# RWKV chunks of a hybrid decoder step: Z and Y formed transposed, group norm by sums on TensorE

## The reference, cut to what matters

```python
def step(state, inp):                       # wkv_scan
    r_t, w_t, k_t, v_t, kk_t, a_t = inp
    s_kk = jnp.einsum('bhvk,bhk->bhv', state, kk_t)
    state = (state * w_t[:, :, None, :] - s_kk[..., None] * (kk_t * a_t)[:, :, None, :]
             + v_t[..., None] * k_t[:, :, None, :])
    return state, jnp.einsum('bhvk,bhk->bhv', state, r_t)
...
mu = jnp.mean(y, axis=-1, keepdims=True)    # over the 64 values of a head
var = jnp.mean(jnp.square(y - mu), axis=-1, keepdims=True)
y = ((y - mu) * lax.rsqrt(var + GN_EPS)).reshape(bsz, t, D_RWKV)
y = y * lw['ln_x_w'].astype(f32) + lw['ln_x_b'].astype(f32)
```

## Time and profile before

| What | Value |
|---|---|
| median of three runs | 2047.21 us |
| the profiled execution's own time | 2051.09 us |
| its span | 2049.3 us |
| TensorE busy, weight loads | 1964.9 us (96%), 1821.8 us (89%) |
| VectorE, ScalarE, GpSimd busy | 988.7 us (48%), 625.6 us (31%), 201.8 us (10%) |
| mean granted TensorE clock | 0.987 |

### The profile page before, as it was taken

One profiled execution on the slowest core, in us unless ns is written; L12 is line 12 of the kernel. 1 busy time (PEld: TensorE's weight loads), 2 busy tenths in 40 slices (PEclk: granted clock), 3 DMA queues, 4 the chain that ended last, 5 costly groups with the idle time before them and its releaser, 6 DMA issues.

```text
span 2049.3 us, 40598 instructions
## 1 busy us (share of the span) xinstructions
PE 1964.9 (96%) x16426; PEld 1821.8 (89%) x16426; DVE 988.7 (48%) x1541; ACT 625.6 (31%) x991; POOL 201.8 (10%) x177
## 2 busy tenths in 40 slices
PE   7999999999999997998898999999999999999997
PEld 7997679999999997965667999999999999999996
DVE  6556766666666665156875644322132222213334
ACT  5114333333332322254545533321032112102213
POOL 0000212222222221221110000000000000000000
PEclk9999999999999998999999999999999999999998
DMA  4213722112232217476564621111111111111112
GB/s 174 84 39 119 262 51 55 49 47 54 60 78 70 74 56 195 150 239 199 167 234 144 232 100 43 50 41 51 42 41 51 41 51 41 45 47 42 51 42 84
DMA packets 111971, 189.45 MB, mean 92 GB/s; under 512 B 62871, under 2 KB 66231, under 8 KB 110407
## 3 DMA queue, kind: packets, MB, share of 16 engines
q1 hardware_dynamic: 109542, 179.15, 27.5%
q10 hardware_dynamic: 2304, 8.50, 1.3%
HBM read 149.83 MB, written 37.79 MB: 92 GB/s over the span
## 4 chain that ended last, share of the span: by engine, by line
PE 72%; issue 14%; DVE 8%; DMA 2%; ACT 2%; POOL 1%; SPq 1%; ACTq 0%; DVEq 0%; POOLq 0%
PE ps L294 44%; PE ps L384 5%; PE ps L386 4%; PE ps L385 4%; PE ps L1022 2%; PE ps L1023 1%; PE ps L1053 1%; DVE arena L1916 1%; DVE arena L1909 1%; PE ps L1210 1%; PE ps L1314 1%; PE ps L1269 1%; DMA normed<-in_kp 1%; PE ps L1136 1%; PE ps L1328 1%
## 5 line engine op out<-in xcount | busy, mean ns | idle before, releaser
L294 PE MATMUL ps<-h_high,wb_split 128*128 128x350 f32 (+1 forms) x1536 | 290.6, 324 | 0.0
L294 PE MATMUL ps<-ff_high,wb_split 128*128 128x350 f32 x1488 | 280.2, 323 | 0.0
L304 ACT CAST wb_split<-weights 128x1024 fp32r<-128x1024 f32 x88 | 92.3, 1049 | 592.7 <-PE ps L294 592.7
L294 PEld LDWEIGHTS ps<-h_high,wb_split 128*128 128x128 f32 x1536 | 254.5, 189 | 0.4
L294 PEld LDWEIGHTS ps<-ff_high,wb_split 128*128 128x128 f32 x1488 | 246.7, 189 | 0.0
L2248 DVE TENSOR_TENSOR arena<-arena,ps 128x1050 f32 (+1 forms) x39 | 48.7, 1249 | 311.1 <-PE ps L294 311.1
L294 PE MATMUL ps<-ff_low,wb_split 128*128 128x350 f32 x744 | 160.6, 324 | 0.0
L2329 POOL TENSOR_TENSOR arena<-arena,constants 64x512 f32<-64x512 f32 x100 | 121.7, 1217 | 332.0 <-DVE arena L1909 322.1
L386 PE MATMUL ps<-fill_high,w_fill_low 128*128 128x350 f32 x468 | 153.4, 328 | 0.0
L2265 DVE SCALAR_TENSOR_TENSOR squares<-ps,arena 128x1050 f32<-128x1050 f32 x32 | 40.1, 1253 | 220.1 <-PE ps L294 209.7
L294 PEld LDWEIGHTS ps<-ff_low,wb_split 128*128 128x128 f32 x744 | 127.0, 189 | 0.0
(11 more groups left out here) (348 smaller groups left out, 3682.4 us busy)
## 6 DMA issues: line engine op xcount, KB each, us to landing
weights<-in_wu SPq DMA_DIRECT2D x122, 512.0 KB, 3.5
normed<-in_vp SPq DMA_DIRECT2D x64, 260.0 KB, 4.6
normed<-in_kp SPq DMA_DIRECT2D x64, 256.0 KB, 4.9
arena<-chunk_dram SPq DMA_DIRECT2D x10, 1248.0 KB, 6.9
arena<-gate_dram SPq DMA_DIRECT2D x16, 525.0 KB, 4.0
chunk_dram<-arena SPq DMA_DIRECT2D x12, 520.0 KB, 5.1
chunk_dram<-fox SPq DMA_DIRECT2D x12, 520.0 KB, 4.6
arena<-samp_dram SPq DMA_DIRECT2D x10, 512.0 KB, 10.6
```

The costliest lines, as they stand in the source:

```text
L294: last = pe.matmul(PS[:, 3 * s + g, 0:n], ws[s][wh][:, k * P:(k + 1) * P], tile_of(x[xh], k)[:, g * G:g * G + n], start=(k == 0 and wh + x ...
L304: act.copy(of[0][s][0], W[:, s]).then_inc(w_hi[s], 1)
```

## The change

Z and Y of a head pair are formed together and transposed (values on partitions). V (104x64) stands and both blocks of MK (208 columns) move; the state stands and [a, r] (208 columns) moves; the two heads of a pair write the two halves of the partitions. Z is copied out (`ZT`) and transposed back to rows in level 4 for u. Y stays in its bank, NU stands and MB1 moves on top of it. Group norm works on transposed Y: ScalarE copies it, TensorE sums over each head's 64 partitions with the block of ones `blk` (416 columns), VectorE centers and squares, TensorE sums again, ScalarE takes Ln and Exp of all 128x416, VectorE scales. `y_back` is gone. The banks of the levels' products move (2, 3 to 4, 5; 4, 5 to 0, 1), because 2 and 3 now hold Z and Y. Two filler steps move from ahead of u to behind it, four stand between the sums, the last four behind them.

```diff
-        Yc = Xm.rearrange("p a b -> p (a b)")
-        gst = r_c2.take(4, NH)
+        ZT, YS_c, SQ_c, RS_c = Lm, E3, Lm, Lc
...
+        LEVELS, ZN_LV = range(1, N_LV), N_LV - 3
...
+                def zy_out(rows, p, x=slice(0, 2)):
+                    at = p % 2 * 2 * C
+                    return PS[rows, 2 + p // 2, at + x.start * C:at + x.stop * C]
+
-                if c:
-                    fill.run(4)
-                    y_back(c - 1)
-                fill.run(12 if c else 8)
+                fill.run(16 if c else 8)
...
                 for h, e, p, rows in by_rows():
-                    pe.matmul(z_out(e, p), MK[0:C, h, 0], Vn[0:C, vcols(h)], start=(p == 0), stop=False,
+                    pe.matmul(zy_out(rows, p), Vn[0:C, vcols(h)], MK[0:C, h].rearrange("p x t -> p (x t)"),
+                              start=(p % 2 == 0), stop=False, skip_group_check=True)
                 for h, e, p, rows in by_rows():
-                    last = pe.matmul(z_out(e, p), AR[rows, p, 0], St[rows, p], start=False, stop=(p == HP - 1),
+                    last = pe.matmul(zy_out(rows, p), St[rows, p], AR[rows, p].rearrange("p a b -> p (a b)"),
+                                     start=False, stop=(p % 2 == 1), skip_group_check=True)
...
+                    if lv == ZN_LV:
+                        wait(ch_act, "z")
+                        wait(ch_dve, f"x_{lv - 1}_0_x")
+                        for p in range(HP):
+                            last = pe.transpose(PS[0:C, 4, p * P:(p + 1) * P], ZT[:, p], ident)
+                        ch_pe.done(last, "zn")
...
+                def head_sums(src):
+                    for e in range(2):
+                        rows = slice(e * HD, (e + 1) * HD)
+                        last = pe.matmul(PS[rows, 0, 0:HP * C], blk[rows, rows],
+                                         src[rows].rearrange("p a b -> p (a b)"), start=True, stop=True)
+                    return last
...
-                fill.run(2)
-                wait(ch_act, "z")
+                wait(ch_act, "zn")
                 wait(ch_dve, f"x_{N_LV - 1}_1_xt")
...
                 ch_pe.done(last, "u")
-                for h, e, p, rows in by_rows():
-                    pe.matmul(y_out(e, p), AR[rows, p, 1], St[rows, p], start=(p == 0), stop=False,
-                for h, e, p, rows in by_rows():
-                    pe.matmul(y_out(e, p), MK[0:C, h, 1], Vn[0:C, vcols(h)], start=False, stop=False,
-                fill.run(2)
-                wait(ch_act, "nu")
-                for h, e, p, rows in by_rows():
-                    last = pe.matmul(y_out(e, p), MB[0:C, h, 1], NU[0:C, h * HD:(h + 1) * HD], start=False,
-                ch_pe.done(last, "y")
+                fill.run(4)
                 for h, e, p, rows in by_rows():
                     pe.matmul(s_out(rows, p), Kn[0:C, vcols(h)], Vn[0:C, vcols(h)], start=(p == 0), stop=False,
+                wait(ch_act, "nu")
+                for h, e, p, rows in by_rows():
+                    last = pe.matmul(zy_out(rows, p, slice(1, 2)), NU[0:C, h * HD:(h + 1) * HD], MB[0:C, h, 1],
+                                     start=False, stop=True, skip_group_check=True)
+                ch_pe.done(last, "y")
...
                 ch_pe.done(last, "s")
+                wait(ch_act, "y")
+                ch_pe.done(head_sums(YS_c), "mean")
+                fill.run(4)
+                wait(ch_dve, "sq")
+                ch_pe.done(head_sums(SQ_c), "var")
                 fill.run()
-                if c == NC - 1:
-                    y_back(c)
```

On ScalarE and VectorE:

```diff
+                act.wait_ge(ch_act.sem, ch_act.before(c))
...
-                ch_act.done(act.copy(Zm[0:C].rearrange("p (e n) -> p e n", e=2), PS[0:C, 2:4, 0:HP * HD]), "z")
+                ch_act.done(act.copy(ZT.rearrange("p (b a) t -> p b a t", b=2), zy_part(0)), "z")
...
+                    if lv == ZN_LV:
+                        wait(ch_pe, "zn")
+                        ch_act.done(act.copy(Zm[0:C], PS[0:C, 4, :]), "zn")
...
+                wait(ch_pe, "y")
+                ch_act.done(act.copy(YS_c.rearrange("p (b a) t -> p b a t", b=2), zy_part(1)), "y")
+                wait(ch_pe, "var")
+                ch_act.done(act.activation(RS_c.rearrange("p a b -> p (a b)"), PS[:, 0, 0:HP * C], ACT.Ln,
+                                           scale=1.0 / HD, bias=par[:, V_GEPS:V_GEPS + 1]), "ln")
                 wait(ch_act, "ln")
+                ch_act.done(act.activation(RS_c, RS_c, ACT.Exp, scale=-0.5), "rstd")
                 out(5)
...
-                wait(ch_pe, "yt")
+                wait(ch_dve, "norm")
                 for p in range(HP):
-                    ch_act.done(act.activation(YTc[:, p], PS[:, 0, p * C:(p + 1) * C], ACT.Identity,
+                    ch_act.done(act.activation(YTc[:, p], YS_c[:, p], ACT.Identity,
...
-                wait(ch_pe, "y")
-                done(dve.tensor_reduce(gst[0:C, 0].rearrange("p (e a) -> p e a", e=2), y, AX.X, ALU.add), "sum")
-                done(dve.tensor_scalar(gst[0:C, 0], gst[0:C, 0], 1.0 / HD, None, ALU.mult), "mean")
+                wait(ch_pe, "mean")
+                done(dve.scalar_tensor_tensor(YS_c, PS[:, 0, 0:HP * C].rearrange("p (a b) -> p a b", a=HP), -1.0 / HD,
+                                              YS_c, ALU.mult, ALU.add), "center")
+                done(dve.tensor_tensor(SQ_c, YS_c, YS_c, ALU.mult), "sq")
                 wait(ch_pe, "s")
...
-                done(dve.tensor_tensor(ych, y, spread4(0), ALU.subtract), "center")
-                done(dve.tensor_tensor(by_head(Zm[0:C]), ych, ych, ALU.mult), "sq")
...
                 wait(ch_act, "rstd")
-                done(dve.tensor_tensor(ych, ych, spread4(3), ALU.mult), "norm")
+                done(dve.tensor_tensor(YS_c, YS_c, RS_c, ALU.mult), "norm")
```

More of the change, by code:

```diff
@@ L597, in build @@
                       + [f"prod_{m}{i}" for i in range(2) for m in "kb"] + ["z"]
[L598 to L601, removed]
+                      + [x for lv in LEVELS for t in ("t1", *(("zn",) if lv == ZN_LV else ()),
+                                                      *(("t2x",) if lv < N_LV - 1 else ()),
+                                                      *(("t2",) if lv >= N_LV - 2 else ()))
+                         for x in ([t] if t == "zn" else [f"{t}_{lv}_{q}" for q in range(2)])]
+                      + ["u", "y", "s", "mean", "var"])
         ch_act = Steps(sem("ch_act"), ["v", "e1", "e3", "e2", "nat_k", "z"]
-                       + [f"t1_{lv}_{q}" for lv in LEVELS for q in range(2)]
-                       + ["nu", "ln", "rstd"] + [f"y_{p}" for p in range(HP)])
+                       + [x for lv in LEVELS for x in [f"t1_{lv}_{q}" for q in range(2)] + ["zn"] * (lv == ZN_LV)]
+                       + ["nu", "y", "ln", "rstd"] + [f"y_{p}" for p in range(HP)])
         ch_dve = Steps(sem("ch_dve"), [f"scan_{p}" for p in range(HP)] + ["lm", "r", "k", "b", "a", "nat_b", "nat_v"]
@@ L610, in build @@
                                           for t in (("xt", "xl") if lv == N_LV - 2 else ("xt",))])]
-                       + ["sum", "mean", "state_sum", "state", "center", "sq", "var", "norm"])
+                       + ["center", "sq", "state_sum", "state", "norm"])
         ch_pool = Steps(sem("ch_pool"), [f"bm_{lv}_{b}" for lv in LEVELS[:-1] for b in ("top", "low")] + ["bonus", "gate"])
@@ L770, in _ @@
             sp.dma_start(A["o_sp"], St).then_inc(sp_stored, 16)
+            sp.wait_ge(ch_act.sem, ch_act.before(NC))
             sp.dma_start(dS.rearrange("p b h k -> p (b h k)"), A["st"]).then_inc(ds_load, 16)
@@ L990, in _ @@
             pe.sem_inc(ch_pe.sem, 1)
[L992 to L996, removed]
             def pe_chunk(c):
@@ L1081, in pe_chunk @@
                     for q in range(2):
-                        wait(ch_act, f"t1_{lv}_{q}")
+                        wait(ch_act, "zn" if lv == ZN_LV else f"t1_{lv}_{q}")
                         if lv > 1:
@@ L1094, in pe_chunk @@
                     for j in range(4):
-                        last = by_halves(4 + q, j, T1, XTr, 4 * q + j)
+                        last = by_halves(q, j, T1, XTr, 4 * q + j)
                     ch_pe.done(last, f"t2_{N_LV - 2}_{q}")
@@ L1567, in act_chunk @@
                             wait(ch_pe, f"{'t2x' if lv < N_LV - 1 else 't2'}_{lv - 1}_{q}")
-                        part = slice(0, C) if lv < N_LV - 1 else low
-                        ch_act.done(act.copy(quad(T1, q)[part], PS[part, q, 0:4 * HB]), f"t1_{lv}_{q}")
+                        part, bank = (slice(0, C), q) if lv < N_LV - 1 else (low, 4 + q)
+                        ch_act.done(act.copy(quad(T1, q)[part], PS[part, bank, 0:4 * HB]), f"t1_{lv}_{q}")
+                    if lv == ZN_LV:
+                        wait(ch_pe, "zn")
+                        ch_act.done(act.copy(Zm[0:C], PS[0:C, 4, :]), "zn")
                     if lv == 4:
@@ L1582, in act_chunk @@
                 out(4)
-                wait(ch_dve, "var")
```

(6 more changed lines are left out.)

42 lines of the change are left out of this document (11 added, 31 removed).

## The result

The changed kernel takes 2057.64 us, the median of 7 runs (2050.73 to 2068.74), against 2047.39 for the kernel before in 7 runs beside it: a ratio of 1.0052, 95% interval 1.0031 to 1.0073. It is slower by half a per cent where 2044.0 was predicted, and lies outside the range of 2037 to 2050.

A forecast was written before the change was run, and what follows sets the result against it. TensorE's own stream was the bound, busy 52.35 of 53.43 us a chunk. Terms of -0.31 a chunk, +0.4 in the first and -1.1 in the last gave -3.2, from median 2047.21 to 2044.0 us; range 2037 to 2050.

The forecast's parts named there:

- D: Ahead of u: two filler steps move behind it, leaving TensorE's wait for VectorE's inverse uncovered, +0.40 us a chunk.
- A: y_back's four transposes go, with their cost on the filler behind: -0.39 us a chunk.
- G: `var`, the second group norm sum: 0.87 us plus 0.14 at the fillers around it, +1.0 us a chunk.
- B: Z's products: 2.40 us becomes 3.16, +0.76, of which waits absorb 0.28 + 0.16, leaving +0.32 a chunk.
- C: Four transposes of Z in level 4: +0.43 us a chunk, nothing added for ScalarE's copy.
- E: Y's first two products go from behind u: -2.36 us a chunk.
- F: Behind the fillers: y, s1, s2 took 2.61 us; with the wait for Y's copy and `mean`, 2.9: +0.29 a chunk.
- rival 4: Column halves don't share the array at 208 columns, in Z and y: 2.1 us a chunk more, 2063 us; chance 0.04.
- The tail's chain: From `var` through norm and scans to Kc: ends under its filler cover, V+9.2 against V+10.5, 1.3 us to spare.
- rival 3: The tail's chain, from Y through norm and scans to Kc, outlasts its cover: slower, 2055 us; chance 0.10.
- Chunk 0: First chunk's tail, VectorE's splits and scans: 8.2 us behind Y instead of 6.9, Y 0.8 to 0.9 earlier: +0.4 us.
- Rival 2: Waits absorb more: B wholly, and the entries of `mean` and `var` hidden: -9 us in all, 2038; chance 0.40.

The follow-up runs named there:

- e8: The changed kernel itself run again, nothing altered: 2054.55 us, ratio 1.0028.
- e1: The changed kernel with two of the four filler steps behind u put back ahead of its waits: 2044.41 us, ratio 0.9972.
- e6: The changed kernel with one filler step ahead of u and three behind it: 2045.55 us, ratio 0.9983.
- e10: The changed kernel with eight extra, unused Kn/Vn products ahead of u's waits: 2050.27 us, ratio 1.0010.
- e5: The changed kernel with two filler steps moved from behind u to ahead of the last level's second products: 2058.33 us, ratio 1.0043.
- e2: The kernel before with only its two filler steps ahead of u moved behind u: 2074.32 us, ratio 1.0129.
- e3: The changed kernel; in chunk 0, y activations and GpSimd's bonus wait for the fifth h_low split: 2058.45 us, ratio 1.0039.
- e4: The changed kernel with the edits of e1 and e3 together: 2043.62 us, ratio 0.9982.
- e7: e1 with one of the last four filler steps moved ahead of `mean`'s wait for ScalarE's copy of Y: 2046.95 us, ratio 0.9994.
- e9: e1 with the Kn/Vn products for the state moved from ahead of NU's wait to behind y: 2042.91 us, ratio 0.9970.

## Why the prediction was wrong

**The step that failed is D.** It said of the two moved filler steps, "This cover is gone and nothing replaces it: +0.40", and priced the wait alone. The wait was sized well: from the last product's start to u it is 0.73 instead of 0.65, so D cost 0.48. What it left out is that TensorE's clock, 1.00 in every steady chunk of before, could fall by such a wait. It fell in 3 of chunks 1 to 8 (2 in e8), at 1.55 us each, and in the last chunk. e1, e6 and e10 have the wait covered in three ways, by two steps, by one and by useless products: no half clock in a steady chunk. The changed kernel, e5 and e2 have it open: 3, 6 and 4. Over all profiles and all ten chunks, a half clock starts 0.4 to 2.5 us behind u's start in 22 of 50 chunks where the wait is open (the changed kernel, e8, e2, e3, e5) and in none of 70 where it is covered (before, e1, e4, e6, e7, e9, e10). This part is shown from both sides. The trace of before could not price it, but it should have been a rival: an engine busy 52.35 of 53.43 us had never been seen to wait half a microsecond behind short products; its longest wait in such a chunk of before is 0.3. The Trainium skill has a like case, of another kernel, in "TensorE: Matmul & The Clock Gate", "A second HAM failure mode: psum-queue depth-cycling": an engine that is often idle for short moments between groups of matmuls has its clock go back and forth. The trace agrees, with an idle 0.50 us and a granted clock of 0.50 about 1.2 us behind u's start; here one such moment in a chunk is enough.

The clock behind u is about half of the miss. The forecast was -3.2 us and the profiles lie +10.0 apart; of the 13.2 between, 4.7 are the three half clocks, 1.8 that of the last chunk, 1.6 lie in chunks 0 and 1, about 1 each in the sum of the steady chunks and in the rest of the last chunk, and 3.0 in code that the change leaves alone.

The other terms, per steady chunk at full clock (us):

| Step | predicted | measured |
|---|---|---|
| A, G and `mean` (y_back gone, `mean`, `var`) | +1.48 | +1.53 |
| B Z and what it absorbs | +0.32 | +0.41 |
| C transposes of Z | +0.43 | +0.40 |
| D the open wait ahead of u | +0.40 | +0.48 |
| E Y's first products gone | -2.36 | -2.35 |
| F without `mean` | -0.58 | -0.60 |
| sum | -0.31 | -0.13, as by the periods |

**B.** Z itself came as worked out, 3.11 for 3.16, and its products of 208 columns at full pace (eight in 1.56), so rival 4 is out: column halves share the array. Z's entry cost 0.09 that the prediction did not charge: the filler ahead is followed after 0.25 (522.00 to 522.25) instead of 0.16 (517.20 to 517.36 before). That the smaller tiles in which Z now begins are the cause is an inference; the prediction charged only the exit and the change in the middle. The waits behind Z took up 0.39 where 0.44 was assumed.

**C, E, F, G** were right within 0.06. The wait ahead of `mean` came as foreseen, and e9 shows that it was avoidable.

**The tail's chain** ended in time, so rival 3 did not happen; that its 2055 lies near the measured 2057.64 is chance. But the 1.3 us to spare were about half that. The chain on VectorE's timeline of the changed kernel, whose `var` starts at 504.67:

```profile
508.14 0.59 DVE L1976 TENSOR_TENSOR arena<-arena 128x416 f32<-128x416 f32 x1 [3.26 <-ACT arena L1597]
509.38 2.35 DVE L1900 TENSOR_TENSOR_SCAN arena<-constants,arena 128x104 f32<-128x104 f32 x4 [0.64 <-DVE arena L1976]
...
514.06 0.59 DVE L1906 TENSOR_TENSOR arena<-arena 128x416 f32<-128x416 f32 x1
```

The norm ends at V+4.06, as worked out (V+4.1). The prediction then let the scan begin at once, "The scans no longer wait for transposes (0.79 idle in the earlier trace rows)"; but a pause of 0.64 stays, with VectorE's own last instruction as its releaser. From the scan to Kc's end it is 5.27 instead of 5.06, since the scans now meet GpSimd. Kc is there at V+9.98 instead of V+9.2, and its transposes start at 515.28, V+10.61. e7, which took one step of 0.48 from this cover, has TensorE wait 0.2 for the next operations of the chain, so what could be spared was about 0.3.

**Chunk 0** was predicted at +0.4 and cost +2.0 together with chunk 1. Its own part was sized right: the scans of its tail end at 294.60 + 1.59 = 296.19, 66.4 behind the first scan, where before it was 65.8. The rest comes in chunk 1. A half clock of 10.2 us reaches over the start of it, 6.8 before; the window of the changed kernel:

```profile
286.65:296.90 10.25, 8.15 (x23) 6.14 (x23) 10.03 (x11) 0.68 (x2) 2.09 (x2) 0.50 0.00 0
```

In e1, with u covered, it is 6.8 again, and first to third scan takes 116.02, the time of before (116.08). But the cover of u does not settle it: e7 has the same cover, 13.7 us of half clock there and 119.02, e6 10.2 and 117.23, e10 10.2 and 117.94, e4 10.2 and 116.21, e9 6.8 and 115.62. By and large the time goes with the length of this half clock, which neither the cover of u nor the late bonus sets. What sets it, and so what the other 1.6 us come from, stays open.

**The last chunk's** tail came as worked out: from `mean` at 773.23 to the last activation's end at 782.03 it is 8.8. The chunk as a whole did not: forecast was -1.1, and it took 1.6 longer, with 1.8 of it for the half clock behind its u; without that it is 0.2 shorter (e1, e3). Timeline of the changed kernel:

```profile
773.23 0.92 PE L1118 MATMUL ps<-arena,constants 64*64 64x416 f32 x4
...
780.46 1.57 ACT L1604 ACTIVATE arena<-arena,params 128x104 f32<-128x104 f32 x4 [0.47 <-DVE arena L1976]
```

**Rival 2** (the waits take more) is out: nothing was absorbed beyond the sum. Of the observations named ahead, the period of 53.1 came as 53.30 in the chunks at full clock, and the waits ahead of u and `mean` stood where foreseen. The sign of being wrong, a period over 53.5, shows in the 54.86 of the others; the clock's row was not among the signs.

**What stays open.** The stretch behind the last y activation, code that is the same in all kernels here, took 1277.3 us in the changed kernel's profile and 1275.5 before. The other profiles lie between 1270.4 and 1278.2, so this part varies by itself and is put down to nothing here. Nor is it shown why only some chunks lose the clock, with the same wait in all ten.

## What to carry to other kernels

Price a wait on a nearly full TensorE twice: its own length, and the clock that it may cost behind it. Before work is moved away from a wait, look for the chunks' granted clock one by one, since a mean of 0.98 hides chunks of 0.97 and of 1.00; and when products must be reordered, let work that is needed anyway stand at the waits (e9), because a filler between small products can pay more for entering and leaving than it hides (e7, at a wait of 0.2; at the wait of 0.5 in e6 it was worth its place). The rewrite was worth having: with two filler steps put back it turns from 0.5% slower into 0.3% faster.

## What the runs showed that was not expected

- One idle half microsecond, ahead of eight short products (sixteen instructions) and behind eight others, in a chunk that is 98% busy, is followed by 3.4 us at the 1.2 GHz level in 2 to 6 of 8 chunks. In the kernel before, uncovered, it is 6.8 to 10.2 us.
- Eight useless products in that half microsecond took the half clocks out of the steady chunks, and the median is 4 to 7 us lower (e10).
- A filler step of 0.48 us between two groups of small products, put where TensorE waited 0.2, added 0.47: nothing was hidden (e7). The Trainium skill, in "TensorEngine Tiling (Array Packing)", Key Properties, has the engine drain at a change of tiling mode. The trace agrees, with 0.25 instead of 0.16 us at Z's entry.
- GpSimd beside VectorE: four scans take 3.14 us where 1.59 is their time without it, and six splits 8.82 for 7.07 (e3 and the changed kernel).
